# Two feed-forward layers: the high half of each weight unit multiplied with both row halves in one 512-column product, the bank emptied in separate steps

## The reference

```python
# first block
h = rmsnorm(x, ffn_norm_w[l])
gate, up = jnp.split(h @ w_gate_up[l], 2, axis=-1)
x = x + (jax.nn.silu(gate) * up) @ w_down[l]
# second block
def conv_ffn(h, w_up, w_dw, b_dw, w_down):
    u = causal_dwconv(h @ w_up, w_dw, b_dw)      # 3 taps along the positions, per column
    val, gt = jnp.split(u, 2, axis=-1)
    return (jax.nn.gelu(gt) * val) @ w_down
```

## Time and profile before

| | |
|---|---|
| median of three runs | 760.95 us |
| span of the profiled execution | 760.4 us |
| between the two | 0.5 us |
| TensorE busy | 743.2 us |
| VectorE busy | 573.7 us |
| ScalarE busy | 399.0 us |
| first feed-forward, from the first product of the gate unit j = 0 to the last down unit | about 192 to 379 us |
| second feed-forward, j = 2 to the last down unit | about 584 to 755 us |

### The profile page before, as it was taken

How to read it: one execution, slowest core, us unless ns; L and a number is a source line. 1 busy time by engine, 2 the same in 40 slices (tenths; PEclk the granted TensorE clock), 3 DMA queues, 4 the chain that set the end, 5 groups by cost and what they waited for, 6 DMA issues and landing times.

```text
span 760.4 us, 13296 instructions
## 1 busy us (share of the span) xinstructions
PE 743.2 (98%) x5256; PEld 684.8 (90%) x5256; DVE 573.7 (75%) x966; ACT 399.0 (52%) x673; POOL 25.2 (3%) x31
## 2 busy tenths in 40 slices
PE   7999999999999999999999999999999999999996
PEld 7988999978999999999889887899889999999995
DVE  5758878776767677678797998977858767676776
ACT  5473445664634443344473444666556565555555
POOL 0031000000000000000003000000010000000000
PEclk9999999999999999999999999999999999999999
DMA  7745354553599888889525523456436655565441
GB/s 300 254 151 167 123 175 159 166 171 107 190 382 345 311 281 278 278 289 376 190 68 192 185 84 112 143 190 197 132 116 206 232 173 172 194 210 172 167 139 56
DMA packets 40526, 148.94 MB, mean 196 GB/s; under 512 B 4496, under 2 KB 4624, under 8 KB 40080
## 3 DMA queue, kind: packets, MB, share of 16 engines
q1 hardware_dynamic: 39600, 142.91, 54.4%
q10 hardware_dynamic: 864, 5.18, 1.8%
HBM read 147.02 MB, written 1.05 MB: 195 GB/s over the span
## 4 chain that ended last, share of the span: by engine, by line
PE 77%; DVE 14%; ACT 4%; issue 2%; DMA 1%; POOL 1%; DVEq 0%; SPq 0%; ACTq 0%
PE bank L1059 14%; PE bank L1062 13%; PE bank L1060 13%; PE bank L1116 6%; PE bank L1117 6%; PE bank L1121 6%; PE bank L1093 4%; DVE wlo L1492 4%; PE bank L1107 3%; PE bank L1253 3%; DVE arena L1498 2%; DVE XN L1498 2%; DVE arena L1492 2%; ACT arena L2077 2%; ACT whi L2077 1%
## 5 line engine op out<-in xcount | busy, mean ns | idle before, releaser
L1059 PE MATMUL bank<-hh,whi 128*128 128x256 f32 x1016 | 290.8, 286 | 0.2
L1062 PE MATMUL bank<-hh,wlo 128*128 128x256 f32 x1016 | 287.5, 283 | 0.8 <-DVE wlo L1492 0.8
L1060 PE MATMUL bank<-hl,whi 128*128 128x256 f32 x1016 | 287.3, 283 | 0.0
L1492 DVE TENSOR_TENSOR wlo<-raw,whi 128x1024 fp32r<-128x1024 f32 x204 | 244.6, 1231 | 26.1 <-ACT whi L2077 26.0
L2077 ACT ACTIVATE whi<-raw 128x1024 fp32r<-128x1024 f32 x204 | 204.2, 1047 | 27.1 <-DMA raw<-w_dram 21.4
L1059 PEld LDWEIGHTS bank<-hh,whi 128*128 128x128 f32 x1016 | 194.6, 192 | 4.5 <-issue 2.2
L1060 PEld LDWEIGHTS bank<-hl,whi 128*128 128x128 f32 x1016 | 194.7, 192 | 1.4
L1062 PEld LDWEIGHTS bank<-hh,wlo 128*128 128x128 f32 x1016 | 194.6, 192 | 1.0 <-DVE wlo L1492 1.0
L1498 DVE SCALAR_TENSOR_TENSOR arena<-bank,cols,arena 128x255 f32<-128x255 f32 (+3 forms) x138 | 58.9, 480 | 28.7 <-ACT arena L2077 27.0
L2077 ACT ACTIVATE arena<-bank 128x256 f32<-128x256 f32 (+2 forms) x75 | 31.9, 445 | 85.0 <-PE bank L1062 65.5
L1117 PE MATMUL bank<-whi,fl 128*128 128x512 f32 x176 | 69.0, 392 | 0.0
(11 more groups left out here) (184 smaller groups left out, 896.9 us busy)
## 6 DMA issues: line engine op xcount, KB each, us to landing
raw<-w_dram SPq DMA_DIRECT2D x268, 512.0 KB, 4.7
arena<-rows_dram ACTq DMA_DIRECT2D x1, 1792.0 KB, 8.2
X<-x_dram SPq DMA_DIRECT2D x2, 512.0 KB, 4.6
arena<-rows_dram ACTq DMA_DIRECT2D x1, 1024.0 KB, 11.7
arena<-bias_dram ACTq DMA_DIRECT2D x1, 1024.0 KB, 15.6
out_dram<-X SPq DMA_DIRECT2D x4, 256.0 KB, 2.0
const<-const_dram ACTq DMA_DIRECT2D x1, 640.0 KB, 3.8
arena<-bias_dram ACTq DMA_DIRECT2D x1, 512.0 KB, 4.7
```

The lines of the kernel that those rows point to most:

```text
L1059: e.matmul(o, a, hh[:, k, :], start=(k == 0), stop=False)
L1060: e.matmul(o, a, hl[:, k, :], start=False, stop=False)
L1062: ins = e.matmul(o, wlo[:, s, k * 128:k * 128 + 128], hh[:, k, :], start=False, stop=(k == 7))
L1492: return e.tensor_tensor(out, a, b, op)
```

## The change

- `hh` and `hl` become two slices of one tensor `hhl` (128 x 8 x 2 x 256), so that slice k of both is one run of 512 columns.
- For j from 2 on, `pair` is replaced by two calls of `joined`, one per unit. Each unit has a bank of its own, banks 6, 7, 0, 1 in turn. Its step `join` runs, for each k, one product of 512 columns (high weights, `hh` and `hl` side by side) and one of 256 (low weights, `hh`, into the left half). The left half then holds high times high and low times high, the right half high times low.
- A new step `whole_row` adds the two halves of a bank: ACT copies the right half to SBUF, DVE adds the left half to it (`ups`, `sil` or `fsum`) and frees the bank.
- What `glu` did for j from 2 on is cut into `first` (ACT: silu, or the tap at distance 0), `shifted` (DVE: two taps of one side; ACT: gelu) and `product` (the multiplication and the two halves). `product` of j - 1 stands between the two units of j. The taps read SBUF in place of PSUM.
- `P.lag` is on from j = 2 to the end of j = 21. At j = 21, the preparation of the last two down units stands behind the steps of the second unit.
- The three tables are issued one by one, at j = 6, 10 and 14.

```diff
+    def joined(name, kind, f, src):
+        P.fill(name, (6, 7, 0, 1)[P.main % 4])
+        P.main += 1
+        i = P.unit("s", kind, f)
+        P.of[i] = (name, 0, src)
+        P.step("join", i, 0)
+        P.step("join", i, 1)
+        P.fills_bank(i, name)
...
         for j in range(FT):
-            if j >= 2:
-                finish(pair(f"u{n}{j}", up, (j, FT + j), ("h", norm)))
-            P.step("glu", n, j)
+            if j == 2:
+                P.lag = True
...
+                joined(f"u{n}{j}_0", up, j, ("h", norm))
+                if j > 2:
+                    P.step("product", n, j - 1)
+                P.step("whole_row", n, j, 0)
+                joined(f"u{n}{j}_1", up, FT + j, ("h", norm))
+                P.step("first", n, j, 0)
+                P.step("shifted", n, j, 0)
+                P.step("whole_row", n, j, 1)
...
+            if n == 1 and j in TABLES:
+                P.step("tables", TABLES.index(j))
+            if j == FT - 1:
+                P.lag = False
             for k in downs(up, j):
                 moving(P.unit("m", down, k), f"d{n}", k, k == 0, False, src=f"f{n}")
+            if j >= 2:
+                P.step("first", n, j, 1)
+                P.step("shifted", n, j, 1)
+            if j == FT - 1:
+                if n == 1:
+                    P.step("product", n, j)
+                P.need(P.next - 1, lead=4)
+        if n == 2:
+            P.step("product", n, FT - 1)
...
+            def join(i, part):
...
+                for k in range(4 * part, 4 * part + 4):
+                    c = slice(k * 128, k * 128 + 128)
+                    if k < 7:
+                        e.matmul(p[:, :], whi[:, s, c], hhl[:, k, :, :], start=(k == 0), stop=False)
+                    w.wait_ge(*P.lo_on[i])
+                    e.matmul(p[:, 0:256], wlo[:, s, c], hh[:, k, :], start=False, stop=False)
+                    if k == 7:
+                        done(i, e.matmul(p[:, :], whi[:, s, c], hhl[:, k, :, :], start=False, stop=True))
...
+            def whole_row(n, j, m):          # VectorE
+                name = f"u{n}{j}_{m}"
+                p = wait_full(name)
+                w.wait_ge("jb", 2 * FT * (n - 1) + 2 * j + m - 4 * n + 1)
+                o = sum_at(n, j, m)
+                freed(tt(o, o, p[:, 0:256], ALU.add), name)
...
+            def whole_row(n, j, m):          # ScalarE
+                p = wait_full(f"u{n}{j}_{m}")
...
+                af(sum_at(n, j, m), p[:, 256:512], ACT.Copy).then_inc(sems["jb"], 1)
```

More of the change, by code:

```diff
@@ L849, in program @@
         XN = sb("XN", [128, 2, 1024])
-        hh = sb("hh", [128, KT, T], F32R)
-        hl = sb("hl", [128, KT, T], F32R)
+        hhl = sb("hhl", [128, KT, 2, T], F32R)
+        hh, hl = hhl[:, :, 0, :], hhl[:, :, 1, :]
         mh = sb("mh", [128, KT, T], F32R)
@@ L1001, in program, with sum_at, taps_before @@
         CONVS = [0, 2, 4, 6, 8, 10]
+        def sum_at(n, j, m):
+            return (ups if m else sil)[:, j % 2, :] if n == 1 else fsum[:, j % 2, m * 256:m * 256 + 256]
+        def taps_before(j):
+            return 3 * min(j, 2) + 4 * max(j - 2, 0)
         block = ctx.enter_context(nc.Block())
@@ L1064, in stat @@
                     done(i, ins)
+            def join(i, part):
+                name, n, (_, norm) = P.of[i]
+                s = place[i] % HL
+                p = open_bank(name) if part == 0 else banks[F[name].bank]
+                w.wait_ge("hi", place[i] + 1)
+                h_ready(norm, part)
+                for k in range(4 * part, 4 * part + 4):
[6 more added lines that the diff above has]
+                        done(i, e.matmul(p[:, :], whi[:, s, c], hhl[:, k, :, :], start=False, stop=True))
             def front(i, _):
@@ L1464, in _ @@
             does = {
-                "start": start, "turn": turn, "stat": stat, "front": front, "whole": whole, "half": half, "movv": movv, "mov": mov, "four": four, "ba": ba,
+                "start": start, "turn": turn, "stat": stat, "front": front, "join": join, "whole": whole, "half": half, "movv": movv, "mov": mov, "four": four, "ba": ba,
                 "turn_ba": turn_ba, "lam": lam_, "norms": norms, "decay": decay, "kk": kk, "kq": kq, "lev_first": lev_first,
@@ L2025, in glu @@
                     return
-                c = fc[:, j % 2, :]
                 for s in (1, 2):
[L2028 to L2035, removed]
+                    for m in range(2):
+                        ins = tap_of(n, j, m, s, p)
                         if s == 2 and m == 1:
@@ L2039, in glu @@
                             ins.then_inc(sems["gd"], 1)
[L2040 to L2042 removed]
+                product(n, j)
             does = {
@@ L2339, in values2, with tables @@
                     af(fh[:, hp, :], o2[hp], ACT.Copy).then_inc(sems["o2h"], 1)
[L2343 to L2347, removed]
+            def tables(n):
+                if n == 0:
+                    wait_full("mod01")
+                    e.dma_start(ROWS, rows_d[0:1, 0:3584].broadcast_to([128, 3584])).then_inc(sems["rows"], 16)
+                elif n == 1:
+                    e.dma_start(GTB, rows_d[0:1, 3584:NROW].broadcast_to([128, 2048])).then_inc(sems["gtb"], 16)
+                else:
+                    e.dma_start(B2, bias2_d[:, :, :]).then_inc(sems["bias2"], 16)
             def glu2(n):
@@ L2413, in glu @@
                     return
[L2414 to L2417, removed]
+                for m in range(2):
+                    first_tap(j, m, p)
                 wait_after(name)
-                af(c[:, 256:512], c[:, 256:512], ACT.Gelu_apprx_tanh).then_inc(sems["gg"], 1)
-                w.wait_ge("gm", j + 1)
-                split_high(2, j, c[:, 0:256])
+                v = fc[:, j % 2, 256:512]
+                af(v, v, ACT.Gelu_apprx_tanh).then_inc(sems["gg"], 1)
+                product(2, j)
             does = {
@@ L2428, in _ @@
                 "glu2": glu2, "qk2": qk2, "gates2": gates2, "mean": mean, "variance": variance, "u2": u2, "co": co,
-                "glu": glu,
+                "glu": glu, "whole_row": whole_row, "shifted": shifted, "product": product, "first": first,
             }
```

75 lines of the change are left out of this document (70 added, 5 removed).

## The result

The changed kernel takes 763.94 us (median of 5 runs, 761.7 to 764.83) beside 760.99 us (5 runs) of the kernel before: ratio 1.0034, 95% interval 1.0024 to 1.0045. The two medians lie 2.95 us apart; the ratio on record, used from here on, makes it slower by 0.34%, 2.6 us. Forecast were 758.2 us, 2.7 us faster, and a range of 754.0 to 762.5; the time lies above it.

What follows compares the result with a forecast made beforehand. The prediction took TensorE's product steps to bound the feed-forwards. 8.3 us saved by merging, 3.1 (layer 1) and 2.5 (layer 2's end) lost: 760.4 - 2.7 = 757.7 us span, plus 0.5 around it, 758.2 us; range 754.0 to 762.5.

Steps and rivals of the forecast that it cites:

- The step of a wide product: Joined units: 512-column step of 0.227 us, narrow one 0.120, saving 0.104 us per unit, 8.3 us in all.
- my 2.3: Joined units: ns saved per slice by merging under the skill's gap rule, 1.5 us in all.
- U10: Layer 1, up unit 20: its low half, made at 27.8 but wanted at 25.8, comes 1.95 us late.
- U7: Layer 1, gate unit 19: low half made at 17.4, wanted at 16.8, so 0.55 us late.
- the dense stretch: Layer 1, j = 17 to 20, a w_ada unit with every gate or up unit: VectorE busy 13.84 of 14.5 us.
- low halves of down units 19 and 20: Layer 2's end: TensorE waits for them behind the last taps, 0.25 us for 19, 2.95 us with both.
- the backlogs on the way: Layer 2: VectorE, needing 7.2 us against TensorE's 5.55, is 1.7 us behind after j = 19, 3.1 after j = 20.
- The tables: Layer 1: issuing the three tables one by one costs 0, bound 1.5 us.
- The 0.5 us: Time outside the span, added to the 757.7 us span to give 758.2 us.
- The rival that ended slower: Joined units: wide step 0.236 to 0.240, saving 0 to 2 us, waits about 5; 764.5 us; chance 0.11 with no-real-change rival.
- my threshold: Wide product's step of 0.233 us, from which the slower rival decides (saving under 4.5 us).
- 0.18: Chance of the rival that low halves are in time, only layer 2's end costing about 1 us: 754.2 us.

Runs made afterwards that it cites:

- e4: Changed kernel, but each joined unit runs its eight 512-column products first, then its eight 256-column ones; ratio 1.0004 to the kernel before.
- e1: Changed kernel with joined units and lag in layer 1 only, layer 2 as in the kernel before; ratio 0.9998 to the kernel before.
- e5: Changed kernel with 20 idle TensorE products before the third of layer 2's last down blocks; ratio 1.0039 to the kernel before.
- e8: Changed kernel with the halves of layer 2's last two down units made before the second side's last taps; one run, layer 2 169.8 us (changed 172.3).
- e11: Changed kernel with the lag never set; ratio 1.0237 to the kernel before, layer 1 172.4 us, layer 2 190.4 us.
- e13: Changed kernel with the lag in layer 2 only; ratio 0.9989 to the kernel before, layer 1 172.5 us, layer 2 170.9 us.
- e6: Changed kernel with layer 2's lag starting at j = 3, not 2; one run, layer 2 171.4 us (changed 172.3).
- e15: Changed kernel with all three tables issued together at j = 2 again; one run, layer 1 179.7 us (changed 175.0).
- e2: Changed kernel with joined units and lag in layer 2 only, layer 1 as in the kernel before; ratio 1.0027 to the kernel before.
- e7: Changed kernel with VectorE's 80 additions cut to one column, sums incomplete; one run, layer 1 173.5 us, layer 2 169.7 us (changed 175.0, 172.3).
- e10: Changed kernel with 10 idle TensorE products before the third of layer 2's last down blocks; ratio 1.0012 to the kernel before.

## Why the prediction was wrong, step by step

Forecast: 8.3 saved, 3.1 and 2.5 lost. Measured in the traces: 5.6 saved; layer 1 shorter by 0.2, layer 2 longer by 2.3, 0.3 more between the layers. The two spans, 760.4 and 761.9, differ by only 1.5 us, since the traced execution of the kernel before took 1.0 us more ahead of the first down unit (204.0 and 203.0 us).

1. **The step of a wide product** is the term that was mis-sized: 0.235 + 0.117 a slice, not 0.227 + 0.120. I took the commonest step of the down units and set the dearer ones aside; they were the nearer rows, since there too something alternates. The joined units save 4.8 us in place of 8.3; with the 0.8 of the down units, which was no term, it costs 2.7 of the 5.3 us between forecast and result (2.7 us faster, 2.6 slower). The formula of the Trainium skill (TensorE: Matmul & The Clock Gate, Back-to-back issue gap), which that section gives for a product by itself, makes an estimate of 216 + 109 ns a slice (merging saves 2.5 ns by it, not my 2.3) and fits neither order; e4's 0.229 + 0.119 is nearest to my figure.
2. **Layer 1**: waits of 3.1 us forecast; 2.8 saved and 0.2 left make 2.6, of which 1.4 us for the low half of up unit 20 (the forecast's U10, 1.95) and 0.7 for down unit 20 (0.55); the first one, at U7, did not come (0.55). In e1, e5 and e8 the loss in the dense stretch falls on two units, 0.5 to 0.9 us each. Place, chain and size were about right. The weight was not: I priced the dense stretch and called the lag a condition, but without the lag (e11, e13) the same dense stretch costs nothing.
3. **The end of layer 2**: 2.95 us forecast for the low halves of down units 19 and 20, 2.7 measured (0.1 and 2.6). The forecast's last taps end 5.4 us after the last up unit; in the trace it is 5.25 (740.87 to 746.12). But the backlogs on the way, 1.7 and 3.1, do not follow from its terms: 7.2 - 5.55 is 1.65 a round, which less the 0.6 in hand makes 1.05 and 2.7. So the number was right, the place and the cause too, and a part of the agreement is luck.
4. **The clock behind that wait** was no term at all: 1.5 us in the profiled execution, and by each run's granted clock in three of the five. I wrote down a wait of 3 us on TensorE and did not ask what it does to the clock.
5. **The start of layer 2**: 0.86 us, no term either. I followed the steady round from j = 3 on and not the first one, where the lag sets in (e6).
6. **The tables**: no cost where they are, as forecast. That they had to be moved I had not seen (e15).
7. **What lies around the span.** The 0.5 us came from two different executions. In the runs here the time is 1.8 to 2.1 us over the span of the same execution. Since the sum was a difference, it did not matter.

The rival that ended slower had the wide step at 0.236 to 0.240 and waits besides, at 764.5 us; with 0.235 it is the case that came, short of my threshold only because alternation makes the narrow step cheaper. I gave it 11 in 100. The points 1, 4 and 5 sum to 5.1 us, all on one side, and the range had 4.3 us above the forecast. The chances were not quite one sum either: 0.18 and three quarters of 0.50 (755.8 to 759.4 of 755.8 to 760.6) are 0.56 for faster, not 0.60.

## What to carry to other kernels

A merged product saves little where the wide product's step is nearly two narrow ones (here 8 ns of a slice's 360, or 12 with wide and narrow ones grouped), so any wait at an end takes it back: follow the first and the last rounds by hand, not just the steady one, and keep the old form there. When work is put one step later to break waits between two engines, it costs a step of lead everywhere it is set, so set it only in the loop that has those waits (layer 2: 18 us longer without it; layer 1: 2.5 us shorter without it).

## What the runs showed of the hardware

- 512 and 256 columns in turn, into one bank with changing weights: 0.235 and 0.117 us a step. Eight of a kind in a row: 0.229 and 0.119. Three of 256 in turn: 0.120 each.
- A TensorE wait of 2.6 us was followed by five to seven products at 1.2 GHz (0.427 in place of 0.227 us) in the traces of the changed kernel, e2 and e6, and by none in those of e4, e7, e13 and e15. With idle products during the wait (e5, e10) no run of 16 had a mean granted clock under 0.998; without them 12 of 31 had 0.997 or less.
- A float32 product of the constant with itself at 128 columns takes 0.22 us, in two records (e10: 20 records from 742.78 to 744.93).
